# A delta-rule layer in which keys and values are turned by VectorE blocks and SBUF-to-SBUF transfers instead of TensorE transposes

## The chip, the cores and the metric

The kernel runs on one core of a Trainium2 chip. The metric is device time in microseconds (us), smaller is better. The kernel before took 1355.09 us (median of 3 runs, 1355.00 to 1355.52). Everything is float32.

## The reference

Two layers over 1152 token positions of width 1024: a prompt of 1024 tokens and eight sampled sequences of 16 tokens. Layer 0 (a linear recurrence beside windowed attention) is not touched. Layer 1 is a gated delta rule with 8 heads of 128 key and 128 value channels. Cut to what matters:

```python
qkv, z, b, a = split(hmod @ w_in)            # 3072 + 1024 + 8 + 8 channels
qkv = silu(causal_dwconv(qkv))               # 4 taps along the tokens
q, k = l2_normalize(q) * 128 ** -0.5, l2_normalize(k)
beta, g = sigmoid(b), -exp(a_log) * softplus(a + dt_bias)
# per chunk: A = (k beta) k^T * decay_strict ; T = (I + A)^-1
w, u, qk = T @ (k beta exp(gcum)), T @ (v beta), (q k^T) * decay_incl
# scan over the chunks
v_new = u - w @ state
o     = (q exp(g)) @ state + qk @ v_new
state = state * exp(g_last) + (k exp(g_last - g))^T @ v_new
y = (rms_norm(o) * silu(z)) @ w_out
```

The kernel writes this for chunks of 128 tokens, which gives the same result: 8 prompt chunks and one that holds all the samples, so 9 in a head.

## The kernel before, in words

The output of the projection lies with channels on the partitions and tokens along them. `S1` holds three such planes of 128x1152 for one head: keys, queries, values (`KEY`, `QUERY`, `VALUE` = 0, 1, 2). Products over channels (`gram_tiles`, `pairs`) take their operands from `S1` directly. Two operands are needed with the tokens on the partitions: `KD` (keys times a decay, nine tiles of 128x128) is the stationary operand of the state update in `scan`, and `VB` (values times a factor `vs`) is the right-hand side of the triangular solve. Before the change TensorE turns them: `transposes` writes 9 tiles of keys (`turn_k` five of them, `extra(1)` in `rest` four) and 9 of values (`extra(6)`, `extra(7)`, `extra(8)`) into PSUM, 18 in each head; VectorE takes them out and scales them, in `keys(h, 0..2)` and `values(h, 0..2)`. A third family of transposes, `outputs`, turns the result back, 9 in a head, and stays.

Each engine has one written program, in which all heads run the same order: `rest(h)` (five rounds of an inverse of 32x32 blocks by powers, then two steps up to 64 and 128), `scan(h)` (eight dependent chunk steps, k = 0 to 7), and then the start of the next head (`gram_k`, on VectorE `front`, `keys`, `norm_q`). Between these dependent pieces stands filler, in 39 numbered places p: on TensorE `fill(h, p)` issues two or three matmuls of the next head's input projection (128x128 by 128x288), whose halves use two PSUM banks in turn; `between(h, p)` on VectorE and ScalarE does the additions, convolution taps and activations that belong to them. `TAIL` is the last four places. The value plane of a head is finished late: its last taps are at p = 0 to 2, ScalarE's tanh at p = 3 and VectorE's `silu(h, VALUE)` at p = 5, that is after the third round of `rest(h)`. The first use of `VB` is the first matmul of `scan(h)`, at k = 0.

SyncE issues every DMA from one queue in written order, and a semaphore wait there holds up all that follows. For head h: the weights of head h + 1, then (after the first step of the scan) the convolution history, the decay rows and the remaining weights, then the sample states. In the last head (h = 7, `ahead` false) it loads `w1out[3]` to `w1out[6]` first, four pieces of 512 KB of the output projection. They lie in the buffers `CV` and `U1` of the convolution; at p = 4 of that head TensorE begins the output projection (`share`), and its first `share` waits for all seven pieces. GpSimd's program for `rest(h)` is: small copies of decays, one weight sum, then, when the fifth round is done, six copies into `XW` and `YF`, in head 0 also the difference `TD4`, and then `head_sums(h + 1, 1)`, the weight sums of the next head's second half.

Of the kernel before, what the change touches and what calls it, by code (L numbers as in the profile page):

```python
# [18 lines left out]
ALU = mybir.AluOpType  # L19
# [3 lines left out]
P = 128  # L23
# [275 lines left out]
def encoder(nc, I, O):  # L299
    ctx = ExitStack()  # L300
    with ctx:
# [173 lines left out]
        TD4 = HT[:, 0:HALF, LO:]  # L475
        zt_half = zt.rearrange("p a t -> p (a t)")[:, 0:LO]
# [36 lines left out]
        def _(sp):  # L513
# [65 lines left out]
            for m in range(LM):  # L579
                if m:  # L580
                    sp.wait_ge(sem("l_mm"), 6 * m)
                sp.dma_start(gw, I["gw"][m]).then_inc(sem("gw_in"), 16)
# [9 lines left out]
            sp.dma_start(wqkv, I["wqkv"]).then_inc(sem("wqkv_in"), 16)  # L592
# [14 lines left out]
            sp.dma_start(kc, I["kc"]).then_inc(sem("kc_in"), 16)  # L607
# [103 lines left out]

            def head(h, ahead):
                if not ahead:
                    for k in range(3, KT - 1):
                        sp.wait_ge(sem("s1_ready"), 3 * H - 2 if k < 5 else 3 * H - 1)
                        sp.dma_start(w1out[k], I["wout"][1, :, k]).then_inc(sem("wout1_in"), 16)
                if ahead:
                    sp.wait_ge(sem("n_ev1"), 7 * h + 4)
# [5 lines left out]
                    weights(h + 1, 3)  # L724
                sp.wait_ge(sem("st_ready"), 8 * h + 1)
                if not ahead:
                    sp.wait_ge(sem("s1_ready"), 3 * H)
                    sp.dma_start(w1out[KT - 1], I["wout"][1, :, KT - 1]).then_inc(sem("wout_in"), 16)
# [66 lines left out]
        def _(pool):  # L795
# [226 lines left out]
            def rest(h, ahead):  # L1022
                wait(pool, sem("kd_ready"), 3 * h + 1)
# [106 lines left out]
        def _(pe):  # L1130
# [159 lines left out]
            def gates(m):  # L1290
                pe.wait_ge(sem("gw_in"), 16 * m + 16)
# [11 lines left out]
                for q in range(2):  # L1303
                    pe.wait_ge(sem(f"w0_in{q}"), 16 * m + 48)
                    project(m, q, "g_mm", lambda n: pe.wait_ge(
# [3 lines left out]
            pe.wait_ge(sem("wqkv_in"), 16)  # L1309
# [93 lines left out]
            def att(t):  # L1403
# [17 lines left out]
                if sample:  # L1421
                    pe.wait_ge(sem("kc_in"), 16)
# [234 lines left out]
            def transposes(bank, m, ks, name, at=0):  # L1657

                for i, k in enumerate(ks):
                    x = tr(at_(bank, at + i), col(m, k))  # L1660
                x.then_inc(sem(name), 1)

# [19 lines left out]
            def turn_k(h):  # L1682
                if not (isinstance(h, int) and h == 0):
                    pe.wait_ge(sem("y1_done"), 3 * h - 1)
                transposes(2, 0, range(4), "tk")
                transposes(4, 0, (8,), "tk")

            def rest(h, ahead):
# [4 lines left out]
                def extra(n):  # L1693
# [4 lines left out]
                    elif n == 1:  # L1698
                        if not first:
                            wait(pe, sem("y1_done"), 3 * h)  # L1700
                        transposes(3, 0, hi, "tk")
                        pe.wait_ge(sem("kd_ready"), 3 * h + 2)
# [3 lines left out]
                    elif n == 3:  # L1706
                        pe.wait_ge(sem("kd_ready"), 3 * h + 3)
# [87 lines left out]
            def scan(h, ahead):  # L1795
                for k in range(8):
# [8 lines left out]
                    else:  # L1805
                        pe.wait_ge(sem("n_ev1"), 7 * h + 7)
                        pe.wait_ge(sem("vb_ready"), 3 * h + 3)
# [17 lines left out]
                    pe.wait_ge(sem("vn_ready"), 8 * h + k + 1)  # L1825
                    mm(at_(6, 2), KD[:, k], VN, start=True, stop=True).then_inc(sem("kv_mm"), 1)
# [1660 lines left out]
```

## Time and profile before

| | |
|---|---|
| median of 3 runs | 1355.09 us |
| profiled execution, span | 1354.8 us |
| TensorE matmul busy | 1325.8 us, 98% |
| TensorE weight load busy | 904.0 us, 67% |
| VectorE busy | 855.6 us, 63% |
| ScalarE busy | 434.6 us, 32% |
| GpSimd busy | 331.1 us, 24% |
| DMA | 111.96 MB in 63297 packets |
| mean granted TensorE clock | 0.997 of full speed |

The span is the time from the first to the last instruction of one profiled execution. Every matmul is issued by one helper line (L1132) and every transpose by another (L1135), so groups of TensorE are told apart by the shape. A matmul of float32 shows as two records, a transpose as one. Busy time of TensorE counts from issue to a modelled end, and records of neighbours overlap: 98% means that it nearly always had something in flight. In the timelines neighbouring instructions of one line are merged in one row. The head's period is read from VectorE's L3188, which runs once in each head: at 671.37, 756.89 and 842.40 us.

### The profile page before, as it was taken

To read this page: it belongs to the slowest core of one execution; us is meant where nothing else is said; L and a number is where in the kernel's file an instruction comes from. 1 tells how busy PE (TensorE), PEld (TensorE's weight loads), DVE (VectorE), ACT (ScalarE), POOL (GpSimd) and SP (SyncE) were. 2 spreads that over 40 slices of the span, in tenths; PEclk is the share of its full clock that TensorE was granted. 3 is DMA by queue.
4 is the path that set the end of the run, shared out by engine and by line. 5 is a ranking of instruction groups with operands and counts; after the bars stand their busy time and mean duration, and the time that the engine had idled before them with its cause. 6 is when DMAs were issued, how large, how long until landed. Compare 5 with 4: busy or idle time off the path is not lost.

```text
span 1354.8 us, 27409 instructions
## 1 busy us (share of the span) xinstructions
PE 1325.8 (98%) x11200; PEld 904.0 (67%) x11200; DVE 855.6 (63%) x1939; ACT 434.6 (32%) x1044; POOL 331.1 (24%) x450
## 2 busy tenths in 40 slices
PE   5999999999999999999999999999999999999997
PEld 3577776666654454667877788877788777875543
DVE  3847874355454375785886858858578586782246
ACT  3213443344431233521422414224143241432221
POOL 1023200010013232523312423224222242212352
PEclk9999999999999999999999999999999999999999
DMA  9531016002034522121212112121121211440124
GB/s 356 235 75 36 5 36 271 8 1 79 3 130 167 195 85 108 13 81 19 71 46 68 34 34 83 38 77 40 34 83 29 75 50 34 127 159 26 35 94 168
DMA packets 63297, 111.96 MB, mean 83 GB/s; under 512 B 34778, under 2 KB 38690, under 8 KB 61618
## 3 DMA queue, kind: packets, MB, share of 16 engines
q1 hardware_dynamic: 63172, 110.21, 24.2%
q8 instruction: 89, 1.46, 0.4%
q14 instruction: 36, 0.29, 0.1%
HBM read 91.79 MB, written 18.40 MB: 81 GB/s over the span
## 4 chain that ended last, share of the span: by engine, by line
PE 88%; DVE 7%; POOL 1%; DMA 1%; issue 1%; ACT 1%; SPq 0%; DVEq 0%; POOLq 0%; ACTq 0%
PE psum L1132 83%; PE psum L1135 5%; DVE mem L2963 1%; DVE mem L2774 1%; DVE mem L3288 1%; DMA mem<-x_dram 1%; DVE mem L3054 0%; DMA y<-mem 0%; DVE mem L3165 0%; DVE mem L2943 0%; DMA mem<-x 0%; POOL mem L954 0%; DVE mem L2780 0%; ACT mem L1915 0%; ACT mem L2087 0%
## 5 line engine op out<-in xcount | busy, mean ns | idle before, releaser
L1132 PE MATMUL psum<-mem 32*32 32x32 f32 (+12 forms) x10592 | 1264.1, 304 | 4.9 <-DVE mem L2475 1.5
L1132 PEld LDWEIGHTS psum<-mem 128*128 128x128 f32 (+4 forms) x10592 | 835.7, 143 | 401.7 <-issue 217.0
L2963 DVE SCALAR_TENSOR_TENSOR mem<-mem 128x576 f32<-128x576 f32 (+1 forms) x126 | 106.1, 842 | 0.0
L1135 PE MATMUL psum<-mem 128*128 128x128 f32 (+1 forms) x608 | 85.1, 278 | 17.2 <-ACT mem L1927 12.9
L1135 PEld LDWEIGHTS psum<-mem 128*128 128x128 f32 (+1 forms) x608 | 70.7, 144 | 41.4 <-issue 21.0
L2278 ACT ACTIVATE mem<-mem 128x128 f32<-128x128 f32 x72 | 22.0, 305 | 127.6 <-DVE mem L3213 74.4
L2164 ACT ACTIVATE mem<-psum 128x288 f32<-128x288 f32 x28 | 11.4, 407 | 104.0 <-PE psum L1132 104.0
L1011 POOL COPY mem<-mem 128x3 f32<-128x3 f32 x24 | 8.4, 348 | 148.9 <-DVE mem L2921 70.1
L2056 ACT ACTIVATE mem<-mem 128x256 f32<-128x256 f32 x72 | 35.5, 495 | 26.4 <-DVE mem L2697 26.4
L2744 DVE TENSOR_TENSOR mem<-mem,psum 128x512 f32<-128x512 f32 x28 | 19.1, 684 | 37.4 <-PE psum L1132 37.0
L2174 ACT ACTIVATE mem<-mem 128x576 f32<-128x576 f32 (+1 forms) x42 | 32.7, 779 | 28.0 <-DVE mem L2941 28.0
L2682 DVE CUSTOM_DVE_ANT_0 mem<-psum,mem 128x256 f32<-128x256 f32 x72 | 26.2, 419 | 23.4 <-PE psum L1132 23.4
L985 POOL TENSOR_TENSOR mem<-mem 128x512 f32<-128x512 f32 x14 | 15.2, 1088 | 103.8 <-issue 93.3
L2087 ACT ACTIVATE mem<-mem 128x1024 f32<-128x1024 f32 x16 | 16.9, 1056 | 71.5 <-DVE mem L2744 30.3
L2204 ACT ACTIVATE mem<-mem 128x1176 f32<-128x1176 f32 x24 | 28.3, 1178 | 30.2 <-DVE mem L2963 30.2
L2987 DVE SCALAR_TENSOR_TENSOR mem<-mem 128x1024 f32<-128x1024 f32 (+1 forms) x31 | 36.7, 1185 | 0.4 <-ACT mem L2204 0.3
L865 POOL TENSOR_TENSOR mem<-mem 128x512 f32<-128x512 f32 x8 | 9.9, 1268 | 109.9 <-DVE mem L2682 108.7
L1927 ACT ACTIVATE mem<-mem 128x1024 f32<-128x1024 f32 x18 | 20.5, 1144 | 48.6 <-POOL mem L806 26.2
L3174 DVE SCALAR_TENSOR_TENSOR mem<-psum,mem 128x128 f32<-128x128 f32 x56 | 19.4, 346 | 25.4 <-PE psum L1132 25.4
L2774 DVE SCALAR_TENSOR_TENSOR mem<-mem 128x1024 f32<-128x1024 f32 x16 | 20.5, 1281 | 19.7 <-POOL mem L856 14.4
L3190 DVE COPY mem<-psum 128x128 f32<-128x128 f32 x64 | 18.4, 287 | 21.0 <-PE psum L1132 20.9
L3205 DVE SCALAR_TENSOR_TENSOR mem<-mem,psum 128x128 f32<-128x128 f32 x56 | 19.2, 344 | 17.1 <-PE psum L1132 17.1
(260 smaller groups left out, 1277.2 us busy)
## 6 DMA issues: line engine op xcount, KB each, us to landing
mem<-modw SPq DMA_DIRECT2D x12, 2048.0 KB, 12.2
mem<-w SPq DMA_DIRECT2D x44, 512.0 KB, 4.3
mem<-x SPq DMA_DIRECT2D x10, 512.0 KB, 4.7
x_dram<-mem SPq DMA_DIRECT2D x9, 512.0 KB, 2.9
mem<-row_dram SPq DMA_DIRECT2D x8, 576.0 KB, 5.2
mem<-x_dram SPq DMA_DIRECT2D x9, 512.0 KB, 3.7
mem<-wout SPq DMA_DIRECT2D x1, 4096.0 KB, 15.0
mem<-gs SPq DMA_DIRECT2D x8, 512.0 KB, 3.6
```

The lines of the kernel that those rows point to most:

```text
L1132: return pe.matmul(*a, **k)
L1135: return pe.transpose(out, in_, ident[0:n, 0:n])
L1927: act.activation(xh[:, slot], XS[:, t % XSLOTS] if l else X[:, t], ACT.Copy, scale=stat[:, 3 * slot + 2:3 * slot + 3]).then_inc(sem("n_xh" ...
L2056: c.mark(act.activation(SS[:, a], SS[:, a], ACT.Exp, scale=HD ** -0.5, bias=nm[:, a:a + 1], accum_out=den[:, a:a + 1]))
L2174: act.activation(CV[:, m, lo:hi], U1[:, m, lo:hi], ACT.Copy, scale=CW[:, 3 * g + ORDER[m], 0:1]).then_inc(sem("pj_ev"), 1)
L2204: act.activation(U1[:, m, PRE:], CV[:, m, 0:UC], ACT.Tanh, scale=0.5).then_inc(sem("th1"), 1)
L2278: x = act.activation(SQJ, OO[:, k], ACT.Square, accum_out=sso[:, k:k + 1])
L2682: i = dve.tensor_tensor_reduce(SS[:, n], B(bk)[:, a * 256:(a + 1) * 256], mask, 1.0, -3.0e38, ALU.add, ALU.max, mx[:, n:n + 1])
L2774: i = dve.scalar_tensor_tensor(two(tmp), src, rs, two(gate[:, w]), ALU.mult, ALU.mult)
L2963: x = dve.scalar_tensor_tensor(cvm, U1[:, m, lo + j:hi + j], CW[:, 3 * g + ORDER[m], j:j + 1], cvm, ALU.mult, ALU.add)
L2987: dve.scalar_tensor_tensor(S1[:, m, a:b], T[:, a:b], 1.0, CV[:, m, a:b], ALU.add, ALU.mult)
L3174: dve.scalar_tensor_tensor(RR, at_(6, 0), HC[:, 1, k:k + 1], VB[:, k], ALU.mult, ALU.add).then_inc(sem("r_ready"), 1)
```

## The change

After the change no TensorE transposes of keys and values are left. In their place: VectorE transposes each plane in 32x32 blocks in one instruction (keys into `KB`, values into `VT`, both in the convolution buffer `CV`); SyncE then moves block row a of each tile to block column a with sixteen SBUF-to-SBUF transfers a plane, each of 32 partitions x 9 tiles x 128 bytes (36 KB); then `KD` is scaled in place by ScalarE (nine instructions of 128x128) and `VB` by GpSimd (one of 128x1152). Several semaphores of layer 0 are merged with others, which changes names and counts only.

```diff
+        KB, VT = CV[:, KEY, 0:TOK], CV[:, VALUE, 0:TOK]
...
             def head(h, ahead):                                   # SyncE
+                sp.wait_ge(sem("kb_ready"), h + 1)
+                if h:
+                    sp.wait_ge(sem("kv_mm"), 8 * h)
+                    sp.wait_ge(sem("sample_mm"), 4 * h)
+                turned(KD, KB, "kd_in")
                 if not ahead:
-                    for k in range(3, KT - 1):
+                    for k in (4, 5, 6, 3):
+                        if k == 3:
+                            sp.wait_ge(sem("kd_in"), 256 * H)
                         sp.wait_ge(sem("s1_ready"), 3 * H - 2 if k < 5 else 3 * H - 1)
                         sp.dma_start(w1out[k], I["wout"][1, :, k]).then_inc(sem("wout1_in"), 16)
                 if ahead:
-                    sp.wait_ge(sem("n_ev1"), 7 * h + 4)
...
+                sp.wait_ge(sem("vt_ready"), h + 1)
+                if h:
+                    sp.wait_ge(sem("o_tp"), 3 * h)
+                turned(VB, VT, "vb_in")
                 sp.wait_ge(sem("st_ready"), 8 * h + 1)
...
+            def turned(dst, src, name):
+                for a in range(4):
+                    for b in range(4):
+                        sp.dma_start(dst[32 * b:32 * b + 32, :, 32 * a:32 * a + 32],
+                                     src.rearrange("p (c t) -> p c t", t=P)[32 * a:32 * a + 32, :,
+                                                                            32 * b:32 * b + 32]
+                                     ).then_inc(sem(name), 16)
...
             def rest(h, ahead):                                   # GpSimd, after the copies into YF (and TD4)
+                wait(pool, sem("vb_in"), 256 * (h + 1))
+                wait(pool, sem("vs_ready"), h + 1)
+                pool.tensor_tensor(VB, VB, bc(vs, 2, P), ALU.mult).then_inc(sem("vb_ready"), 1)
                 if ahead:
                     head_sums(h + 1, 1)
...
-            def turn_k(h):                                        # TensorE
-                if not (isinstance(h, int) and h == 0):
-                    pe.wait_ge(sem("y1_done"), 3 * h - 1)
-                transposes(2, 0, range(4), "tk")
-                transposes(4, 0, (8,), "tk")
...
                     elif n == 1:
                         if not first:
-                            wait(pe, sem("y1_done"), 3 * h)
-                        transposes(3, 0, hi, "tk")
-                        pe.wait_ge(sem("kd_ready"), 3 * h + 2)
+                            wait(pe, sem("y1_done"), 3 * h - 1)
                         pairs(4, 0, 1, (8,), "gq_mm", 2)
...
                     elif n == 3:
-                        pe.wait_ge(sem("kd_ready"), 3 * h + 3)
+                        if not first:
+                            wait(pe, sem("y1_done"), 3 * h)
                         pairs(3, 0, 0, hi, "gram_mm")
...
-                    elif n == 6:
-                        pe.wait_ge(sem("umf_ready"), 2 * h + 2)
-                        pe.wait_ge(sem("s1_ready"), 3 * h + 3)
-                        transposes(3, 2, lo, "tv")
-                    elif n == 7:
-                        pe.wait_ge(sem("eq_ready"), 3 * h + 2)
-                        transposes(4, 2, hi, "tv")
-                    else:
-                        pe.wait_ge(sem("eq_ready"), 3 * h + 3)
-                        transposes(2, 2, (8,), "tv")
...
+            def scaled_keys(h):                                   # ScalarE, after between(h, 5)
+                wait(act, sem("kd_in"), 256 * (h + 1))
+                wait(act, sem("kb_ready"), h + 1)
+                for k in range(NT):
+                    i = act.activation(KD[:, k], KD[:, k], ACT.Copy, scale=kdc[:, k:k + 1])
+                i.then_inc(sem("kd_ready"), 1)
...
-            def keys(h, n):                                       # VectorE
-                a, b, src = ((0, 4, four(2)), (8, 9, four(4, 0, 1)), (4, 8, four(3)))[n]
-                dve.wait_ge(sem("tk"), 3 * h + n + 1)
-                if n == 0:
-                    c.sync()
-                dve.tensor_tensor(KD[:, a:b], src, bc(kdc[:, a:b], 2, P), ALU.mult
-                                  ).then_inc(sem("kd_ready"), 1)
+            def keys(h):
+                dve.wait_ge(sem("s1_ready"), 3 * h + KEY + 1)
+                dve.transpose(KB, S1[:, KEY]).then_inc(sem("kb_ready"), 1)
...
+            def values(h):                                        # VectorE, at p == 5 right after silu(h, VALUE)
+                dve.wait_ge(sem("s1_ready"), 3 * h + VALUE + 1)
+                dve.transpose(VT, S1[:, VALUE]).then_inc(sem("vt_ready"), 1)
```

## Rows read from the trace of the kernel before

**Rows 1.** The page: busy time by engine, and the chain that ended last by engine
```profile
PE 1325.8 (98%) x11200; PEld 904.0 (67%) x11200; DVE 855.6 (63%) x1939; ACT 434.6 (32%) x1044; POOL 331.1 (24%) x450
...
PE 88%; DVE 7%; POOL 1%; DMA 1%; issue 1%; ACT 1%; SPq 0%; DVEq 0%; POOLq 0%; ACTq 0%
```

**Rows 2.** Busy time in one head's period: stretch, its length, engines, clock, DMA, GB/s
```profile
671.37:756.89 85.52, 85.08 (x1071) 67.46 (x1070) 63.21 (x147) 27.04 (x75) 24.05 (x38) 1.00 0.19 54
```

**Rows 3.** TensorE's transposes in that period: busy, mean ns of one | idle before
```profile
L1135 PE MATMUL psum<-mem 128*128 128x128 f32 x27 | 4.2, 275 | 0.3 <-DVE mem L3165 0.3
```

**Rows 4.** Chain of waits, 690 to 725: start, us, what
```profile
692.09 0.66 PE psum L1135 x4
...
708.47 0.44 PE psum L1135 x4
708.91 1.46 PE psum L1132 x6
```

**Rows 5.** VectorE's timeline at the start of a head: start, us, instruction [idle before]
```profile
681.95 0.46 DVE L3032 TENSOR_TENSOR mem<-psum,mem 128x288 f32<-128x288 f32 x1 [0.19 <-PE psum L1132]
...
686.34 0.89 DVE L3054 TENSOR_TENSOR mem<-psum,mem 128x512 f32<-128x512 f32 x2
...
690.93 0.48 DVE L3092 STREAM_TRANSPOSE mem<-mem 128x288 f32<-128x288 f32 x1
...
700.21 0.22 DVE L3105 TENSOR_TENSOR mem<-mem,psum 128x64 f32<-128x64 f32 x1 [1.82 <-PE psum L1132]
```

**Rows 6.** VectorE's timeline from the value plane to the scan's first copy
```profile
703.33 2.15 DVE L2987 SCALAR_TENSOR_TENSOR mem<-mem 128x1024 f32<-128x1024 f32 x1
705.41 0.28 DVE L2993 SCALAR_TENSOR_TENSOR mem<-mem 128x128 f32<-128x128 f32 x1
706.45 0.46 DVE L3112 TENSOR_TENSOR mem<-mem,psum 128x288 f32<-128x288 f32 x1 [0.77 <-PE psum L1132]
...
723.03 0.29 DVE L3190 COPY mem<-psum 128x128 f32<-128x128 f32 x1 [0.37 <-PE psum L1132]
```

**Rows 7.** SyncE's timeline: issues of small transfers, alone and close together
```profile
556.38 0.43 SPq L686 DMA_DIRECT2D mem<-lmask  x1
556.85 0.43 SPq L687 DMA_DIRECT2D mem<-ident  x1
...
726.31 1.64 SPq L676 DMA_DIRECT2D mem<-cs  x3
727.99 2.14 SPq L699 DMA_DIRECT2D mem<-row_dram  x1
```

**Rows 8.** The page's DMA issues: KB each, us from issue to landing
```profile
mem<-wout SPq DMA_DIRECT2D x8, 512.0 KB, 5.9
...
mem<-cs SPq DMA_DIRECT2D x28, 12.0 KB, 2.4
...
mem<-lmask SPq DMA_DIRECT2D x4, 20.0 KB, 1.8
```

**Rows 9.** GpSimd's timeline: the difference of head 0, and the copies into YF of head 2
```profile
629.84 5.05 POOL L1046 TENSOR_TENSOR mem<-mem 128x2304 f32<-128x2304 f32 x1
...
713.48 1.81 POOL L1040 COPY mem<-mem 32x288 f32<-32x288 f32 x4
```

**Rows 10.** ScalarE's timeline: four 128x128 scalings, and its copy of round 4
```profile
684.61 1.28 ACT L2239 ACTIVATE mem<-mem 128x128 f32<-128x128 f32 x4 [0.61 <-DVE mem L3042]
...
705.83 0.41 ACT L2250 ACTIVATE mem<-psum 128x288 f32<-128x288 f32 x1 [2.21 <-PE psum L1132]
```

**Rows 11.** Last head: SyncE's four loads
```profile
1197.62 2.30 SPq L716 DMA_DIRECT2D mem<-wout  x4
```

**Rows 12.** Last head: VectorE's timeline at its key copies and its third round
```profile
1197.25 0.89 DVE L3054 TENSOR_TENSOR mem<-psum,mem 128x512 f32<-128x512 f32 x2
...
1209.16 0.21 DVE L3105 TENSOR_TENSOR mem<-mem,psum 128x64 f32<-128x64 f32 x1
```

**Rows 13.** Busy time and DMA rate while those loads move
```profile
1199.00:1205.00 6.00, 5.76 (x113) 4.47 (x99) 5.90 (x13) 0.69 (x1) 0.00 (x0) 1.00 1.02 408
```

More of the change, by code:

```diff
@@ L1022, in rest @@
             def rest(h, ahead):
-                wait(pool, sem("kd_ready"), 3 * h + 1)
+                wait(pool, sem("kb_ready"), h + 1)
                 c.mark(pool.tensor_copy(HC, HCn[:, 1:3]))
@@ L1290, in gates @@
             def gates(m):
-                pe.wait_ge(sem("gw_in"), 16 * m + 16)
+                pe.wait_ge(sem("proj_in"), 16 * m + 16)
                 pe.wait_ge(sem("xc_ready"), m + 1)
@@ L1655, in gram_tiles @@
                 return x
[L1657 to L1661, printed above, removed]
             def pairs(bank, m, n, ks, name, at=0):
@@ L1825, in scan @@
                     pe.wait_ge(sem("vn_ready"), 8 * h + k + 1)
+                    if k == 0:
+                        pe.wait_ge(sem("kd_ready"), h + 1)
                     mm(at_(6, 2), KD[:, k], VN, start=True, stop=True).then_inc(sem("kv_mm"), 1)
@@ L1989, in lru @@
                     if m and i == 0:
-                        wait(act, sem("l_a"), m)
+                        wait(act, sem("l_act"), 2 * m - 1)
                     elif m and i == 3:
@@ L2005, in lru @@
                 wait(act, sem("l_w"), m + 1)
-                act.activation(lw_, lw_, ACT.Sqrt).then_inc(sem("l_sq"), 1)
+                act.activation(lw_, lw_, ACT.Sqrt).then_inc(sem("l_act"), 1)
                 if m == LM - 1:
                     for g in range(6):
-                        wait(act, sem("g_mm"), g + 1)
+                        wait(act, sem("xa_mm"), 6 + g + 1)
                         wait(act, sem("g_ev"), G_LAST + g - 1)
@@ L2170, in first_tap @@
                 wait(act, sem("s1_ready"), 3 * (g - 1) + m + 1)
+                if m == KEY:
+                    wait(act, sem("kd_in"), 256 * g)
+                elif m == VALUE:
+                    wait(act, sem("vb_in"), 256 * g)
                 if n:
@@ L2253, in rest @@
                     between(h, 2 * r - 1, ahead)
+                    if r == 3:
+                        scaled_keys(h)
                 between(h, 8, ahead)
@@ L2596, in chain @@
             def chain(m):
-                dve.wait_ge(sem("l_a"), m + 1)
+                dve.wait_ge(sem("l_act"), 2 * m + 1)
                 dve.wait_ge(sem("lz_ev"), 6 * m + 6)
@@ L2607, in chain @@
                     added(m + 1, "u2")
-                dve.wait_ge(sem("l_sq"), m + 1)
+                dve.wait_ge(sem("l_act"), 2 * m + 2)
                 c.sync()
@@ L3026, in between @@
                     silu(h, VALUE)
+                    values(h)
             def front(h):
@@ L3067, in norm_q @@
                        sem("ssq_ready"), h + 1)
-            def values(h, n):
-                a, b, src = ((0, 4, four(3)), (4, 8, four(4)), (8, 9, four(2, 0, 1)))[n]
-                dve.wait_ge(sem("tv"), 3 * h + n + 1)
-                if n == 0:
-                    dve.wait_ge(sem("vs_ready"), h + 1)
-                dve.tensor_tensor(VB[:, a:b], src, bc(vs[:, a:b], 2, P), ALU.mult
-                                  ).then_inc(sem("vb_ready"), 1)
+            def values(h):
+                dve.wait_ge(sem("s1_ready"), 3 * h + VALUE + 1)
+                dve.transpose(VT, S1[:, VALUE]).then_inc(sem("vt_ready"), 1)
             def queries(h, n):
@@ L3129, in rest @@
                         queries(h, 2)
-                    else:
-                        values(h, 1)
                     between(h, 2 * r - 2, ahead)
@@ L3135, in rest @@
                             norm_q(0)
-                        keys(h, 2)
                     elif r == 2:
@@ L3140, in rest @@
                         queries(h, 1)
-                    elif r == 4:
-                        values(h, 0)
-                    else:
-                        values(h, 2)
                     if r < 5:
@@ L3236, in head @@
                     between(h, TAIL + 1, ahead)
-                    keys(h + 1, 0)
-                    keys(h + 1, 1)
+                    keys(h + 1)
                     between(h, TAIL + 2, ahead)
@@ L3260, in _ @@
                         conv(7, j)
-            keys(0, 0)
-            keys(0, 1)
+            keys(0)
             for h in range(H - 1):
```

25 lines of the change are left out of this document (13 added, 12 removed).

## The prediction

> **What bounds the kernel now.** I read the page's busy times and its chain first: TensorE has something in flight for 98% of the span and holds 88% of the chain that ended last, VectorE 7% [rows 1]. Then the stretches: in a head's period of 85.52 us TensorE is busy for 85.08, VectorE for 63.21, and the granted clock is 1.00, the upper of its two levels (2.4 GHz) [rows 2]. So the delta layer costs about what TensorE's instruction stream costs, and each instruction taken from it is worth its issue interval, not its duration. The groups show the difference: 27 transposes in the period, mean 275 ns each, yet 4.2 us of busy time in all [rows 3]. The chain gives the interval: 0.44 us for four in a row, so 0.11 for one; a record of a filler matmul takes 1.46 / 6 = 0.24 [rows 4].
>
> The Trainium skill (Perfetto Trace Analysis, "Identifying the Most-Contended Engine") says that matmul busy time is a poor measure of TensorE's load and weight-load busy time a better one; that stands at 67% here. By that rule TensorE would have slack, and removed transposes would be worth nothing. What bears against it is in the chain, which by the next paragraph leaves TensorE only at the head's start.
>
> There VectorE is the one that is late. From 681.95, when it stops waiting for TensorE, it works without a gap, and TensorE waits for its L3165 until 692.09 [rows 4, 5], by 0.3 us on the matmul side [rows 3]. VectorE first idles again at 700.21 [rows 5]. After that TensorE leads through the rest of the period: VectorE waits at 706.45 and at 723.03 [rows 6].
>
> **The change part by part**, for head 2 (671.37 to 756.89), in the clock of the kernel before.
>
> Key transposes. Nine go, 9 x 0.11 = 0.99 us, and with them the wait on L3165 (0.3), now needed only two places later: at most 1.3. But VectorE sets the end here. Its two copies `keys(h, 0)` and `keys(h, 1)` took 0.89 [rows 5]. The block transpose of 128x288 took 0.48 [rows 5]. The one of 128x1152 is not in this trace. Bounds: four times the small one, 1.9, and from below the 0.89 that those copies took for 640 columns. VectorE's pace is (0.46 - 0.29) / (288 - 128) = 0.00106 us for a further column (L3032 and L3190) [rows 5, 6], which makes 0.48 + 864 x 0.00106 = 1.4; I take that, since a long instruction is mostly streaming. So VectorE comes 0.5 us later to the round-1 transpose, which ended at 691.41 [rows 5] and now ends at 691.9. TensorE's second round starts then. Before, it started at 692.09 + 0.44 + 0.22 (one pair, two records of a size like a transpose) = 692.75. Gain 0.8 us at each of the seven starts that have a head before them, 5.6. With a transpose of 1.9 us it is 0.3 each, 2.1. Head 0 has TensorE in the lead, so all nine count: 1.0.
>
> Value transposes. Nine in `rest`, where TensorE leads: 0.99 x 8 heads = 7.9 us. `values(h)` puts 1.4 us on VectorE after `silu`, which ended at 705.69 [rows 6]; 0.8 earlier plus 1.4 gives 706.3. The queue behind it is round 4 (L3112 at 706.45, or 705.65 with the gain) [rows 6], so that starts 0.65 late. TensorE has six filler matmuls of two records each between rounds 4 and 5 (12 x 0.24 = 2.9 us) [rows 4], which cover it. If the cover fails it costs 0.7 us a head.
>
> Getting `VB` in time. This is the new path: block transpose done 706.3, sixteen DMA issues, landing, one GpSimd multiplication, then TensorE's first matmul of the scan. That one ran just before VectorE's copy at 723.03 [rows 6], at about 722.6; with 1.8 us gained it wants `VB` at 720.8.
> - Issue: small transfers follow each other at 0.47 us (556.38, 556.85) [rows 7], three with many 12-byte pieces at 0.55, and the next behind those took 2.14 [rows 7], so (1.64 + 2.14) / 4 = 0.95 is the bound above. Each new one has 288 pieces of 128 bytes; the `lmask` one has 160 of that size and is the nearest row. I take 0.47: the last is issued at 706.3 + 15 x 0.47 = 713.4.
> - Landing: 1.8 us for `lmask`, 2.4 for `cs` [rows 8]. I take 2.1: 715.5. No transfer from SBUF to SBUF is in the trace; the same pair serves as bounds.
> - GpSimd: its copies end at 715.3, less the gain, so it is free [rows 9]. 128x2304 took 5.05 us [rows 9], so 128x1152 takes about 2.6: `VB` is ready at 718.1.
> That leaves 2.7 us: nothing is added. The decisive number is the issue interval: at (720.8 - 2.6 - 2.1 - 706.3) / 15 = 0.65 us the slack is gone, and at 0.95 TensorE waits 4.5 us in each head.
> Behind this wait on GpSimd stand the weight sums `head_sums(h + 1, 1)`, which TensorE's filler first wants at place 25, in the scan's fifth step, some 15 us later. On SyncE, history and rows wait for the scan's first state anyway; the loads of weights in front lose a wait and go earlier.
> In head 0 the difference `TD4` (5.05) stands ahead of the multiplication [rows 9]: it ended at 634.89, now about 1 us earlier, plus 2.6 is 636.5. TensorE wants `VB` at 722.6 less a period of 85.5 less the 2.0 of its 18 transposes, 635.1. Cost 1.4 us, once.
>
> `KD`. Block transpose ends at 686.34 + 1.4 = 687.7, the sixteen issues at 695.2, landed 697. ScalarE scales after place 5, nine at 0.32 = 2.9 us [rows 10], from about 702.6 to 705.5; behind it stands its copy for round 5, at 705.83 [rows 10], used only some 3 us later. `KD` itself is first read in the scan. Nothing added; at 0.95 a transfer it lands at 704.1, and the copy would be 2 us late, still inside the cover.
>
> The last head. SyncE issues the keys' sixteen transfers ahead of the four `wout` loads. Before, these were issued from 1197.62 [rows 11] and moved at 408 GB/s in a stretch that ended near 1206 [rows 13]. Now `KB` is ready at 1197.25 + 1.4 = 1198.6 [rows 12], the transfers are out at 1206.2, the first three loads at 1207.4, and the fourth waits for the keys to land, 1208.1. Four times 524 KB at 408 GB/s is 5.1 us, so all have landed at about 1213.2. TensorE's first `share` comes right after round 3, whose result VectorE took at 1209.16 [rows 12], so at 1209.0, less 0.8: 1208.2. It waits 5.0 us, once. Bounds: 2.5 us if most of the loads overlap the keys' transfers, 9 with slow issues.
>
> Sum: -5.6 - 1.0 - 7.9 + 1.4 + 5.0 = -8.1 us. The profiled span 1354.8 becomes 1346.7; the median stands 0.3 above the span, so 1347.0.
>
> **A rule that speaks against it.** Small transfers close together overlap in this trace: each landed 1.8 us after its issue while the next was out 0.47 us later [rows 7, 8]. The Trainium skill (DMA: Bandwidth & Descriptors, "Rules for kernel authors") says to coalesce many small transfers, since under 64 KB one pays mostly overhead. With the fixed 2.0 us that its section on the anatomy of one DMA gives for the GpSimd path, taken one after the other, a plane would need some 32 us and each head would lose about 20, an estimate. The first rival below goes the same way, by rows.
>
> **The rivals.**
> 1. `VB` late, slower. Place: TensorE's first matmul of every scan. Price: the issue interval above 0.65 us, times 15. For it: the pieces are 128 bytes on both sides, nearly twice as many as in the nearest row, and 2.14 us behind the `cs` burst [rows 7]. Against: `lmask` has the same piece size and kept 0.47. At 0.8 us each: landing at 720.4, ready 723.0, 2.2 us in each of eight heads (18 more, less the 1.4 that head 0 has anyway), and 5 more in the last head: 1347 + 16 + 5 = 1368. At 0.95: 1347 + 35 + 7 = 1389.
> 2. Everything hidden. The loads of the last head overlap, and VectorE's longer chain does not show: 15.8 us for 144 transposes and up to 2.1 for seven waits, less the 1.4 of head 0: 1338 to 1341. For it: TensorE's 98%. Against: VectorE's chain at the start has no idle time to give [rows 5].
> 3. TensorE doesn't lead, as the weight-load share suggests: the gains of the value part vanish in waits between rounds. -5.6 - 1.0 + 1.4 + 5.0 = -0.2, about 1355, and 1353 to 1357 with a part of them kept or a wait added.
>
> **How the numbers follow.** My forecast, 1347 with its own range of 1342 to 1352: 0.57. Rival 1: 0.24, slower than before from about 0.70 us an issue on. Rival 2: 0.10. Rival 3: 0.09, of it 0.08 within 0.2% (2.7 us, about what a measurement of this kernel can tell from no change). The mild end of rival 1 and the slow end of the forecast give the same again or less. Faster 0.67, same 0.09, slower 0.24. The range: 1339 to 1371, which leaves about 0.1 above and little below.
>
> **What would show it.** The period of L3188 falls from 85.5 to 83.7 us. SyncE's row of sixteen issues is 7.5 us long, 9.5 at most. TensorE has no wait on GpSimd at the scan's first matmul except in head 0, and one of about 5 us before the first `share`. The second round's start follows VectorE's L3092 directly. The forecast is wrong if a plane's transfers take over 10 us from first issue to landing plus 2, if the block transpose takes over 2 us, or if the period does not shrink.

## The result and the profile after

The changed kernel takes 1363.55 us (median of 4 runs, 1362.64 to 1368.9) against 1355.3 in the same session. The ratio is 1.007, with a 95% interval of 1.0053 to 1.0088: slower. 1347.0 was forecast, faster.

The page of the changed kernel, answering to [rows 1]:

```profile
PE 1311.3 (96%) x11056; PEld 889.1 (65%) x11056; DVE 852.5 (63%) x1907; ACT 455.0 (33%) x1116; POOL 352.4 (26%) x458
...
DMA packets 141122, 121.41 MB, mean 89 GB/s; under 512 B 112602, under 2 KB 116514, under 8 KB 139442
...
PE 82%; DVE 5%; issue 4%; SPq 3%; DMA 2%; POOL 2%; ACT 0%; POOLq 0%; DVEq 0%; ACTq 0%
```

TensorE has lost 144 records and 14.5 us of busy time, and the span has still grown by 7.2 us (8.3 by the medians: the traced execution of before is 1.5 us longer than its usual ones, as shown below). SyncE's queue, 0% of the chain before, holds 3% of it, which is some 40 us. The waits of TensorE (us in total, times, longest) name what took the gain:

```profile
PE psum L1156 <- DMA mem<-wout: 11.6, 1, 11.6
PE psum L1156 <- POOL mem L1070: 9.0, 6, 2.3
```

L1156 issues the matmuls and L1070 is GpSimd's scaling of `VB`. In before's trace TensorE waits for neither. Both waits begin at SyncE. Its timeline in head 2 (as the prediction calls the second of the eight, h = 1) and in the last head, a plane's sixteen transfers in a row:

```profile
685.93 12.11 SPq L717 DMA_DIRECT2D mem<-mem  x16
...
704.29 12.06 SPq L717 DMA_DIRECT2D mem<-mem  x16
...
1194.33 12.82 SPq L717 DMA_DIRECT2D mem<-mem  x16
1207.20 2.03 SPq L733 DMA_DIRECT2D mem<-wout  x4
```

and one issue by itself (ns, min/median/max), where [rows 7] had 0.43 us for `lmask`:

```profile
L717 SPq DMA_DIRECT2D mem<-mem x256: 585/613/1797, 601.1 to 1234.8; - x128
```

Most take 0.61 us and one to four in each plane 0.7 to 1.8, so that a plane costs 10.9 to 12.8 us, 11.9 in the mean, or about 0.75 a transfer. The long ones have a companion in the trace. All 27 issues over 1 us overlap a 16 KB transfer of the queue that the page calls `instruction` (q8, the loading of code), and most of them end 0.4 us behind its end. Of the 224 issues up to 0.7 us only 28 overlap one. One of the long issues, and the DMA view of 707 to 708:

```profile
707.55 1.11 SPq L717
...
q8 instruction: 1, 0.02, 6.0%
```

The chain of waits in head 2 (start, us, what) shows how that reaches TensorE:

```profile
702.88 1.39 DVE mem L3087
704.27 0.02 issue
704.29 0.60 SPq L717
...
711.29 6.63 issue
...
717.97 2.09 POOL mem L1070
720.06 0.14 issue
720.20 4.04 PE psum L1156 x30
```

GpSimd has nothing to do for 6.6 us and starts when the last transfer has landed. The same view for the last head, and then TensorE around that stall (stretch, length, busy, granted clock, DMA share, GB/s):

```profile
1208.33 0.43 SPq L733
...
1208.86 6.33 DMA mem<-wout
1215.18 0.14 issue
1215.32 14.74 PE psum L1156 x179
```
```profile
1194.00:1204.00 10.00, 9.64 (x249) 1.00 0.52 133
1204.00:1215.30 11.30, 0.00 (x0) 0.69 0.61 202
1215.30:1219.00 3.70, 3.68 (x7) 0.56 0.00 0
1219.00:1223.00 4.00, 4.00 (x101) 1.00 0.00 0
```

After the stall TensorE runs at half the clock, the lower of its two levels, until 1218.5. For 3.2 us of work that costs another 1.6 us (an estimate).

Where the time went, by the start of the line that [rows 2] runs between (L3188, now L3193), the head's mark:

| | before | after | kernel without transfers (e1) |
|---|---|---|---|
| start to head 0's mark | 671.4 | 669.8 | 667.5 |
| six middle periods, mean | 85.2 | 84.7 | 82.9 |
| last period | 90.2 | 101.3 | 89.7 |
| last mark to the end | 82.3 | 82.5 | 82.1 |

The third mark of before is at 841.98, not at 842.40 as said above: of its periods the first is 85.5 us and the other five are 85.1.

2.0 us of the first row belong to none of the heads, nor to the change. Near the start TensorE has a wait of 0.5 us for VectorE, which is the same in every kernel. It ends at 47.35 in before's trace, at 45.39 in the changed kernel's and at 45.23 in e1's. Before's execution had its first load later (TensorE's first wait ends at 10.33 instead of 9.44) and then a stretch at half the clock:

```profile
25.90:29.30 3.40, 3.00 (x5) 1.82 (x6) 1.42 (x4) 2.39 (x5) 0.75 (x3) 0.50 1.02 430
```

e2's execution has such a stretch too, and 19 other executions of before have a median span of 1353.3 us, not 1354.8. From the end of that wait to head 0's mark it is 624.0 us before, 624.4 after and 622.3 in e1.

The price of the transfers by the medians is 1363.6 - 1338.8 = 24.8 us. The waits for `VB` (9.0), the one for `wout` (11.6) and the half clock behind it (1.6) make 22.2. What is left is spread: middle periods less their waits are still 0.2 to 0.4 us above e1's. Its cause stays open.

### The profile page after: what moved, and what is told of

Its sections match the earlier page's. It is cut to its first block, busy times and chain, and to the rows that moved or that the text cites. A ratio compares the mean times of both kernels' runs of the same rounds, so it can differ in the third digit from the quotient of the medians.

```text
span 1362.0 us, 27447 instructions
## 1 busy us (share of the span) xinstructions
PE 1311.3 (96%) x11056; PEld 889.1 (65%) x11056; DVE 852.5 (63%) x1907; ACT 455.0 (33%) x1116; POOL 352.4 (26%) x458
## 4 chain that ended last, share of the span: by engine, by line
PE 82%; DVE 5%; issue 4%; SPq 3%; DMA 2%; POOL 2%; ACT 0%; POOLq 0%; DVEq 0%; ACTq 0%
PE psum L1156 79%; PE psum L1159 3%; SPq L717 3%; DMA mem<-modw 2%; POOL mem L1070 1%; DVE mem L3002 1%; POOL mem L1061 1%; DVE mem L3070 1%; DVE mem L3087 1%; DMA mem<-wout 0%; DVE mem L2978 0%; POOL mem L1067 0%; DVE mem L3094 0%; DVE mem L3061 0%; DVE mem L3058 0%
## 5 line engine op out<-in xcount | busy, mean ns | idle before, releaser
L1156 PE MATMUL psum<-mem 32*32 32x32 f32 (+12 forms) x10592 | 1261.6, 304 | 29.6 <-DMA mem<-wout 11.6
L1156 PEld LDWEIGHTS psum<-mem 128*128 128x128 f32 (+4 forms) x10592 | 837.4, 143 | 435.0 <-issue 244.6
L1159 PE MATMUL psum<-mem 128*128 128x128 f32 (+1 forms) x464 | 62.6, 279 | 14.1 <-ACT mem L1928 12.2
L1159 PEld LDWEIGHTS psum<-mem 128*128 128x128 f32 (+1 forms) x464 | 53.3, 145 | 30.0 <-issue 18.6
L2165 ACT ACTIVATE mem<-psum 128x288 f32<-128x288 f32 x28 | 11.5, 409 | 95.4 <-PE psum L1156 95.4
L2759 DVE TENSOR_TENSOR mem<-mem,psum 128x512 f32<-128x512 f32 x28 | 19.2, 685 | 37.3 <-PE psum L1156 36.9
L1006 POOL TENSOR_TENSOR mem<-mem 128x512 f32<-128x512 f32 x14 | 15.2, 1089 | 89.1 <-issue 79.6
L2789 DVE SCALAR_TENSOR_TENSOR mem<-mem 128x1024 f32<-128x1024 f32 x16 | 20.5, 1281 | 18.8 <-POOL mem L877 14.7
```

The lines of the kernel that those rows point to most:

```text
L1156: return pe.matmul(*a, **k)
L1159: return pe.transpose(out, in_, ident[0:n, 0:n])
L2789: i = dve.scalar_tensor_tensor(two(tmp), src, rs, two(gate[:, w]), ALU.mult, ALU.mult)
```

## The experiments

My theory: the transposes were worth what the prediction says or more, but sixteen issues in a row hold SyncE's queue for 12 us instead of 7.5, and this (a) makes `VB` late and (b) puts the last head's `wout` loads far behind TensorE. Rivals: TensorE doesn't lead; the DMA engines and not the queue are the limit; the pieces and not the transfers set the issue time.

**e1, no transfers.** VectorE writes the turned 32x32 blocks straight into `KD` and `VB` (float32 as before, though the text below calls the planes bf16). The blocks stay where they are, so this kernel's results are other ones, as are those of e3, e5 and e10:

```
-                turned(KD, KB, "kd_in")
-                turned(VB, VT, "vb_in")
-                dve.transpose(KB, S1[:, KEY]).then_inc(sem("kb_ready"), 1)
+                dve.transpose(flat(KD), S1[:, KEY]).then_inc(sem("kb_ready"), 1)
```
(the values likewise; the waits for the transfers go)

> VectorE turns the 32x32 blocks of keys and values straight into the bf16 planes and no SBUF-to-SBUF transfer is issued; the blocks stay where they are, so the planes hold values in other places and the arithmetic is that of other numbers. 144 TensorE transposes are gone, as in the changed kernel, and SyncE's queue is that of before. Theory A (TensorE's work sets the end; the SyncE queue took the gain back): the periods of the middle heads fall by the prediction's 0.8 + 0.99 = 1.8 us, the end of the last head stays as before, and the time is 1355.3 - 14.5 to 16 = 1339 to 1341 us. Theory B (the transposes lie in holes of TensorE, so that taking them out gives nothing): 1353 to 1356 us. Theory C (only the keys' transposes, ahead of an empty pipeline, count): 1347 to 1349 us.

1338.8 us, ratio to before 0.9872 (0.9857 to 0.9887). Theory A. Its period, which answers to [rows 2]:

```profile
667.50:750.40 82.90, 82.67 (x1053) 65.75 (x1052) 62.46 (x142) 29.55 (x84) 26.69 (x39) 1.00 0.19 55
```

Its six middle periods lie between 82.90 and 82.97. So 18 transposes a head are worth 2.2 us there. In the last head only 0.5 us show. There TensorE has a stall of 1.3 us at 1190.13 for which the profile shows no releaser.

**e2, the last head's loads first.**

```
+                if not ahead:
+                    for k in (4, 5, 6):
+                        sp.wait_ge(sem("s1_ready"), 3 * H - 2 if k < 5 else 3 * H - 1)
+                        sp.dma_start(w1out[k], I["wout"][1, :, k]).then_inc(sem("wout1_in"), 16)
                 sp.wait_ge(sem("kb_ready"), h + 1)
...
                 turned(KD, KB, "kd_in")
...
+                q = (0, 1, 2, 4, 5, 6, 3)[k]
```

> The changed kernel, but in the last head three of the four wout loads stand ahead of the keys' sixteen transfers in SyncE's queue, and the fourth, which needs the place of the weights' last reader, behind them; TensorE takes that tile last. Theory A (the last period's extra 11 us is wout issued 12.8 us later): TensorE's 11.6 us wait for wout falls to under 1.5 us, the last period falls from 101.3 to 90 to 92 us, and the time is 1363.6 - 10 = 1352 to 1355 us. Theory B (the last head is slow because the transfers of 128-byte pieces crowd wout's own transfer on the DMA engines, whatever the order): the landing grows by several us, and the time is 1359 to 1363 us.

1351.7 us, ratio 0.9972 (0.9958 to 0.9987): this edit alone makes the change a gain. The last period is 91.2 us, and TensorE waits:

```profile
PE psum L1158 <- POOL mem L1071: 5.9, 6, 1.7
...
PE psum L1158 <- DMA mem<-wout: 1.8, 1, 1.8
```

Theory A, though the wait that is left is 1.8 us where under 1.5 was said, and the time is just below its range. Three of the four loads went forward, and the fourth stays behind the keys. Of the 11.8 us, 10.1 are in the last period. The rest is in heads that this edit doesn't touch: the same program waited 9.0 us for `VB` in the one execution and 5.9 in the other. Such waits are compared below with that in mind.

**e3 and e10, what makes an issue slow.** Sixteen transfers and 36 KB each stay. e3 takes 32 pieces of 1152 bytes, e10 all 128 partitions and 128 pieces of 288:

```
e3  +  sp.dma_start(dst.rearrange("p c t -> p (c t)")[32 * b:32 * b + 32, 32 * NT * a:32 * NT * (a + 1)],
    +               src[32 * a:32 * a + 32, 32 * NT * b:32 * NT * (b + 1)])
e10 +  sp.dma_start(dst.rearrange("p c t -> p (c t)")[:, n:n + 72], src[:, n:n + 72])
```

> The changed kernel with the same 16 transfers a plane of 36 KB each, but every one made of 32 pieces of 1152 bytes instead of 288 of 128; the data land in other places of the planes, so the arithmetic is that of other numbers. Theory A (what a transfer costs SyncE grows with the number of its pieces): one issue goes from 0.65 us (585 to 1797 ns) to the 0.47 us of the cs, lmask and ident loads, a plane from 12.1 to 7.5 us, the wait for the values' plane (9.0 us in sum over six heads) is gone, the last head's wait falls from 11.6 to about 7, and the time is 1347 to 1351 us. Theory B (a transfer from SBUF to SBUF costs SyncE 0.65 us whatever its pieces, or a queue of sixteen backs up): the issue stays at 0.6 to 0.7 us, and the time is within 1361 to 1364 us.

> The changed kernel with the same 16 transfers of 36 KB a plane, but each from all 128 partitions to the same 128, 72 columns wide (128 pieces of 288 bytes); the arithmetic is that of other numbers. Theory A (a transfer from SBUF to SBUF costs SyncE 0.6 us and more, whatever its shape): the issue stays at 0.59 to 0.61 us, a plane at 11 to 12 us, and the time is 1358 to 1364 us. Theory B (what makes the issue slow is that 32 partitions are read and 32 written): one issue takes 0.43 to 0.47 us as those of the loads from DRAM, a plane takes 7.5 to 8 us, the values' plane is in time, and the time is 1347 to 1351 us.

e3: 1358.2 us (ratio 1.0018, 1.0009 to 1.0027); e10: 1360.0 (1.0036, 1.0019 to 1.0053). Their issues:

```profile
L717 SPq DMA_DIRECT2D mem<-mem x256: 507/591/1748, 601.9 to 1227.0; - x128
```
```profile
L718 SPq DMA_DIRECT2D mem<-mem x256: 465/601/1804, 601.1 to 1230.8; - x128
```

A ninth of the pieces takes 0.02 us off the median, and 0.7 us off a plane in the mean of all sixteen (11.2 instead of 11.9; e10: 11.4). The long ones stay, and again all of them overlap a load of code. For e3 theory B is near: the shape matters little. Its time lies between both forecasts, and its waits for `VB` are 3.6 us instead of 9.0 or 5.9: near the edge of the slack a little less counts for much. For e10 theory A.

**e5, four transfers instead of sixteen**, with the same 4608 pieces of 128 bytes in a plane:

```
+                    sp.dma_start(dst[:, :, 32 * a:32 * a + 32],
+                                 src.rearrange("p (c t) -> p c t", t=P)[:, :, 32 * a:32 * a + 32]
```

> The changed kernel with 4 transfers a plane instead of 16: each moves all 128 partitions of a quarter of the columns, 1152 pieces of 128 bytes, so bytes and pieces of a plane are what they were, and the partitions stay, so the arithmetic is that of other numbers. Theory A (SyncE pays by the transfer, some 0.65 to 0.75 us each): a plane takes 2.6 to 3.0 us of the queue instead of 12.1, the values' plane is never late (9.0 us back), wout is issued 9 us sooner (its 11.6 us wait falls to 2 or 3), and the time is 1342 to 1347 us. Theory B (SyncE pays by the piece): one issue grows to 2.5 to 3 us, the plane stays at 11 to 12 us, and the time is 1360 to 1364 us. Theory C (the DMA engines are what a plane waits for): the issues are short and the landing grows to 8 us or more, and the time is 1350 to 1360 us.

1347.2 us, ratio 0.9935 (0.9922 to 0.9949). TensorE waits for GpSimd nowhere, the middle periods are 82.9 us as in e1, and `wout` costs 6.0 us. SyncE's planes in head 2, and one issue:

```profile
685.41 3.44 SPq L716 DMA_DIRECT2D mem<-mem  x4
...
703.76 3.08 SPq L716 DMA_DIRECT2D mem<-mem  x4
```
```profile
L716 SPq DMA_DIRECT2D mem<-mem x64: 595/744/3166, 602.5 to 1209.2; - x64
```

Four times the pieces in a transfer raise its median from 0.61 to 0.74, so a plane falls to a quarter. Theory A, at the slow edge of its range. As equal bytes in equal pieces are in time here, the DMA engines were not the limit for `VB` (that the partitions stay doesn't matter, by e10). The landing grew from 2.1 to 3.8 us, which is hidden there. In the last head it is not: one issue took 3.2 us, and the fourth load waits for the keys' landing (4.0 us), so that TensorE's wait is 6.0 us where 2 to 3 was said.

**e4 and e9, the keys alone.** The values go back to TensorE's transposes, with `wout` behind the keys (e4) or ahead of them (e9):

```
-                turned(VB, VT, "vb_in")
+                    elif n == 6:
+                        pe.wait_ge(sem("umf_ready"), 2 * h + 2)
+                        pe.wait_ge(sem("s1_ready"), 3 * h + 3)
+                        transposes(3, 2, lo, "tv")
```
(and the rest of `values(h, n)` as before)

> The keys are turned by VectorE and sixteen transfers as in the changed kernel; the values go through TensorE's transposes and VectorE's scaled evictions as in the kernel before. Theory A (the values' transfers give back per head what their transposes gained, and the keys' the last head's wait): no wait for the values' plane, the middle periods are 85.1 - 0.8 = 84.3 us, the last period is 90.2 - 0.8 + 11 = about 100 us, and the time is 1355.3 - 6.6 + 11 = 1359 to 1361 us. Theory B (it is the values' transfers that delay the last head): the last period is under 92 us, and the time is 1348 to 1351 us.

> Only the keys are turned by VectorE and sixteen transfers, the values go through TensorE's transposes as before, and in the last head three wout loads stand ahead of the keys' transfers. Theory A (the values' plane is the one that a slow queue makes late, the keys' is in time once wout is out of its way): the middle periods are 83.9 us as with the keys alone, TensorE's 11.5 us wait for wout is gone, and the time is 1359.7 - 11 = 1347 to 1350 us, below the 1351.7 of the version that turns both with sixteen transfers: turning the values so loses. Theory B (the keys' transfers have a price of their own in the last head beside wout): 1352 us or more.

e4: 1359.7 us, ratio 1.0031 (1.002 to 1.0042), periods of 83.9 us but one (85.7, with a stall of 1.6 us without a releaser), the last 102.6, and

```profile
PE psum L1148 <- DMA mem<-wout: 11.5, 1, 11.5
```

Theory A. e9: 1350.5 us, ratio 0.996 (0.9945 to 0.9974), just above A's 1350; the last period is 90.9, but one middle period is 87.6 (last section). That turning the values too (e2, 1351.7) loses against leaving them is not shown: they were measured apart, and their ratios to before (0.9972 and 0.996) have intervals that overlap. What is shown: with sixteen transfers the values gain nothing that can be measured, and in the changed kernel's order of loads they lose: 1363.55 us against e4's 1359.7, with ratios whose intervals lie apart.

**e6, two queues.** Half of the values' transfers from ScalarE, on top of e2:

```
+                for a in (2, 3):
+                    for b in range(4):
+                        act.dma_start(VB[32 * b:32 * b + 32, :, 32 * a:32 * a + 32], ...)
                 wait(act, sem("w_mm"), L + 2)
```

> The kernel with the wout loads ahead of the keys' transfers, and half of the values' sixteen transfers issued by ScalarE, which idles for 6 us there, beside SyncE's half. Theory A (the plane is late by the time that one queue needs for sixteen issues): the values' plane lands some 6 us sooner, TensorE's wait for GpSimd's scaling (5.9 us in six heads) is gone, each middle period is at most 84 us, and the time is 1351.7 - 6 to 8 = 1344 to 1346 us. Theory B (two queues share what makes the issues slow, so that 8 beside 8 take as long as 16): 1350 to 1352 us. Theory C (ScalarE's eviction behind the issues comes late): a wait of TensorE for ScalarE appears, and the time is above 1352 us.

1349.95 us, ratio 0.9954 (0.9942 to 0.9967). The wait for GpSimd is gone, and another stands in its place:

```profile
703.59 6.84 ACTq L2289 DMA_DIRECT2D mem<-mem  x8
710.48 0.38 ACT L2294 ACTIVATE mem<-psum 128x256 f32<-128x256 f32 x1 [7.49 <-issue]
```
```profile
PE psum L1167 <- ACT mem L2294: 3.7, 5, 1.0
```

SyncE's eight took 5.9 us beside it, 0.74 each as when alone, so theory B's mechanism falls, though its 1350 is the nearest number. But the long issues are shared: in each of the first seven heads both queues have one at the same time, and both end within 0.02 us (in head 2, SyncE's 1.28 us at 708.84 and ScalarE's 1.63 us at 708.83). Theory C's mechanism came with a total that A and C both missed: ScalarE's eight issues took 6.8 us of a hole of 6.1, and the eviction behind them, for the inverse's step up to 64, came late by up to 1 us.

**e7 and e8, the changed kernel's planes with fewer issues**, both on top of e2. e7 writes the plane to DRAM and reads it back in four; e8 lets GpSimd copy the four blocks of the diagonal and issues twelve:

```
e7 +                sp.dma_start(t_dram[n], src).then_inc(sem(f"t_out{n}"), 16)
   +                sp.wait_ge(sem(f"t_out{n}"), 16 * (h + 1))
   +                for b in range(4):
   +                    sp.dma_start(dst[32 * b:32 * b + 32].rearrange("p c (a t) -> p c a t", t=32),
   +                                 t_dram[n].rearrange("(a p) (c b t) -> b p c a t", p=32, b=4, t=32)[b])
e8 -                    for b in range(4):
   +                    for b in (b for b in range(4) if b != a):
   +                for q in range(4):
   +                    r = slice(32 * q, 32 * q + 32)
   +                    pool.tensor_copy(dst[r, :, r], src.rearrange("p (c t) -> p c t", t=P)[r, :, r])
```

> The kernel with the wout loads ahead of the keys' transfers, and each plane turned through DRAM: one transfer writes it out, four read it back in pieces of 128 bytes, 5 issues instead of 16. Theory A (the number of issues is what costs): issues 5 times 0.65 and two landings of 2.1 us make 7.5 us from VectorE's transpose to the last landing instead of 14.2, the values' plane is not late, and the time is 1344 to 1347 us. Theory B (the trip through DRAM costs more than eleven issues): the landings are 4 us and more each, the plane is as late as before or later, and the time is 1351 us or more.

> The kernel with the wout loads ahead of the keys' transfers; the four blocks on each plane's diagonal, which need no change of partition, are copied by GpSimd, and 12 transfers a plane are left. Theory A (the queue's time is by the transfer): a plane takes 9 us of the queue instead of 12.1, the values' plane is 3 us sooner, half or more of TensorE's 5.9 us wait goes, and the time is 1346 to 1349 us. Theory B (GpSimd's eight small copies a head push its other work back): TensorE or VectorE waits for GpSimd, and the time is 1351 to 1356 us.

e7: 1341.3 us, ratio 0.9893 (0.9878 to 0.9908), middle periods of 82.9. e8: 1341.4, 0.9891 (0.9878 to 0.9905), middle periods of 83.0 to 83.3. Theory A in both, and better than it said. For e7 the way to it was longer than theory A had it: from the first issue in head 2 to the last landing it is 10.6 us, not 7.5, since the write takes 2.8 to land and the reads 4.1. That is still in time. The values' planes in head 2, e7 and then e8:

```profile
702.71 0.33 SPq L718 DMA_DIRECT2D t_dram<-mem  x1
705.53 3.89 SPq L724 DMA_DIRECT2D mem<-t_dram  x4
```
```profile
702.64 9.41 SPq L717 DMA_DIRECT2D mem<-mem  x12
```

In e8 GpSimd's scaling starts at 713.62, 11.0 us after SyncE's first issue, and in after 13.7. Those 2.7 us are more than `VB` was ever late (2.3); its copies (2.3 us a plane) fell into idle time.

**e11, through DRAM, but `wout` last:** e7's transfers on the changed kernel's order of loads.

> Both planes turned through DRAM in 5 issues, and the last head's wout loads left behind the keys' plane, as in the changed kernel. Theory A (the late wout is a matter of how long the queue is held, and its wait costs TensorE's clock besides): the queue is held from the keys' transpose for 0.4 us, a landing of 2 to 3 us and four issues of 3.4 us, some 6.5 us instead of 12.8; TensorE waits 5 to 6 us for wout instead of 11.6, the middle periods stay at 82.9 us, and the time is 1341.3 + 4 to 6 = 1345 to 1347 us. Theory B (with the planes' traffic out of the way, wout's place in the queue no longer matters): 1341 to 1342 us.

1350.0 us, ratio 0.9955 (0.994 to 0.997). I had expected 1345 to 1347. SyncE is at `wout` 10.0 us after the keys' transpose instead of 12.9, but in the last head the write to DRAM takes 6.5 us to land, where it is 2.8 to 4.4 for the keys elsewhere, and the four `wout` loads take 3.8 us to issue. TensorE waits 10.1 us, and then it runs at half the clock:

```profile
1192.00:1202.00 10.00, 0.40 (x1) 0.59 0.79 241
1202.00:1208.00 6.00, 6.00 (x15) 0.55 0.00 0
1208.00:1215.00 7.00, 7.00 (x184) 1.00 0.22 86
```

Half the clock until 1207.4 costs 2.9 us here (an estimate) where the changed kernel lost 1.6, so the last period, 101.0 us, is nearly as long as its 101.3. So it is loads queued behind a plane, and not the sixteen issues in themselves, that this head cannot bear.

**e12, the best of each:** keys as in e8, values as in e7.

> wout ahead of the keys' transfers; the keys turned by 12 transfers and GpSimd's four diagonal copies, the values through DRAM in 5 issues. Theory A (each plane is in time, and what is left above the kernel without transfers are GpSimd's copies of the values, 0.24 us a period, and the last head's landing of the keys behind wout in DRAM, 1.4 us): 1339.5 to 1341 us. Theory B (what is left has nothing to do with how the planes travel): 1341.3 us as with either alone.

1339.1 us, ratio 0.9879 (0.9864 to 0.9894): below both kernels of the case and level with e1 (which has that stall of 1.3 us). Its last period is 89.1 us, no wait for `wout` appears, and the middle periods are 83.0 to 83.3. So theory A's number was nearly met and both of its terms were wrong. The 1.4 us in the last head are not there, and the 0.2 us a period are, though the values go as in e7. They come with the keys' way, twelve transfers and GpSimd's copies. Which of the two it is was not separated.

## Why the prediction was wrong

The failed step is one line of "Getting `VB` in time": issue interval "I take 0.47", from the `lmask` row. It measured 0.65 with its gap, and 0.75 with the long ones. The text gave 0.65 as the point where the slack is gone. That interval entered twice. Beside it the sum put the half clock behind the last head's wait at nothing, without a reason: 1.6 us.

- `VB`. In time since the head's mark: forecast 34.9 us for the block transpose's end, 44.1 for the last landing, 46.7 for `VB` ready, 49.4 for TensorE's need. Measured in head 2: 34.5, 48.2, 50.3 and 48.9 (720.20 less the wait of 1.5). The last issue comes 11.5 us behind the first instead of 7.1, landing was right (2.1), GpSimd's multiplication was 0.5 shorter than said. TensorE waited 9.0 us in six heads where 1.4 in one was forecast. e5 and e7 take the cause away, and their middle periods are e1's.
- Head 0. The forecast 1.4 us, for `TD4` ahead of the multiplication, were 1.7, but that is luck: GpSimd waited for the transfers. Without them (e1) the multiplication follows `TD4` at once and TensorE doesn't wait. After, then e1:

```profile
633.14 2.11 POOL L1070 TENSOR_TENSOR mem<-mem 128x1152 f32<-128x1152 f32 x1 [1.66 <-DMA mem<-mem]
...
630.88 2.11 POOL L1058 TENSOR_TENSOR mem<-mem 128x1152 f32<-128x1152 f32 x1
```
- The last head. Forecast 5.0 us, bounds 2.5 to 9, measured 11.6. From the mark: `KB` ready 16.2 against 16.1, TensorE there 25.8 against 25.5, `wout` landed 30.8 against 36.9. Of these 6.1 us, 5.2 are the issues (12.8 instead of 7.6). The bound "9 with slow issues" was too low by its own rows: at 0.95 us each sixteen issues take 7.7 us more than at 0.47, which with the 5.0 makes 12.7. e2 returns 10.1 us in that period.
- Key transposes. Forecast 0.8 us a head; e4's periods of 83.9 against 85.1 make it 1.2. The block transpose was right (1.4 forecast, 1.37 measured). But VectorE did not come 0.5 us later to the end of round 1's transpose. It ended 20.0 us behind the mark before, 20.5 by the forecast and 20.25 after; the block transpose started 0.2 us sooner than the copies did. That is 0.3 of the 0.4 us:

```profile
689.52 0.48 DVE L3104 STREAM_TRANSPOSE mem<-mem 128x288 f32<-128x288 f32 x1
```
- Value transposes. Forecast 0.99 us a head; 83.9 (e4) less 82.9 (e1) is 1.0.
- TensorE leads. Right: e1's 1338.8 is the rival "everything hidden" (1338 to 1341), 16.6 us below before. 144 issue intervals are 15.8, and the waits for VectorE at the heads' starts fell from 2.0 to 1.4, so the removed instructions were worth their issue interval. The weight-load share of 67% did not mean slack.
- `KD`. Nothing was added in the middle heads, as forecast: with the keys alone (e4) TensorE waits for no plane.
- Rival 1 named place and mechanism, with a chance of 0.24. Its price at 0.8 us each was 1368, against 1363.6 at 0.75. Its wait of 2.2 us in each of eight heads was too high, since only six waited, by 0.4 to 2.3; the last head's 5 more was near the 6.6 more that were measured. So the place and the order of size of what came stood in the text. What was wrong is the side of 0.65 us on which the number was put.

The Trainium skill (DMA: Bandwidth & Descriptors, "Rules for kernel authors") says to coalesce many small transfers. The runs agree on the transfers: from sixteen (e2) to five (e7) is 1351.7 to 1341.3 us. They don't agree with my use of it, where landings follow one another: each landed 2.1 us after its issue while the next was issued 0.65 us later, and it was the issues that could not overlap.

What I should have seen in the rows: the `cs` burst had 0.55 us and 2.14 behind it, the `lmask` row 0.43, and `VB`'s slack ended at 0.65. The 2.14 (727.99 to 730.13) overlaps a load of code too, so it was a sign of the long ones. With a decisive number that sits inside its own bounds, 0.24 for the far side is too little, and the same number decides the last head too.

## What to carry to other kernels

Here a small SBUF-to-SBUF transfer cost its queue about 0.6 to 0.75 us in each of four shapes, so count the issues in a row and set that time, not the landing, against the slack of who waits. Before a burst goes into a queue, look at every load behind it in every head: the one exceptional head had 11.6 us of waiting and 1.6 us of half clock here, `VB` 9.0 us of waiting in all the others together. Work taken off the leading engine is worth its interval, but only as long as what replaces it has less latency than the slack.

## What the runs showed of the hardware

- SyncE's issue of a transfer from SBUF to SBUF takes 0.59 to 0.61 us in the median for 32, 128 or 288 pieces, and 0.74 for 1152, with single ones up to 2.1 (3.2 for 1152). A plane written to DRAM in 128 pieces of 4608 bytes was issued in 0.33, but twice in 1.3 to 1.5 in e7's last head. What sets 0.6 against 0.33 and the 0.43 of small loads from DRAM stays open.
- Issues over 1 us go with loads of code: 27 of 27 in the changed kernel, 24 of 24 in e2 and in e3, 25 of 25 in e10 and in e8 overlap a 16 KB transfer of the `instruction` queue. Which engine's code it is, and how it holds SyncE up, no run shows. TensorE's stalls of 1.0 to 1.9 us without a releaser (e1, e4, e9 and others) also begin within 0.6 us of the end of such a load.
- A stall of 1.9 us on TensorE was followed in e9 by 3.4 us at half the clock, and that period took 87.6 us instead of 83.9: twice what the stall itself cost. The stall of 1.6 us in e4 had no such stretch behind it, and its period took 85.7.

```profile
954.40:956.40 2.00, 0.13 (x10) 0.05 (x1) 0.00 (x0) 0.22 (x1) 0.00 (x0) 1.00 0.00 0
...
957.80:961.20 3.40, 3.40 (x11) 2.55 (x10) 1.78 (x3) 0.00 (x0) 0.00 (x0) 0.50 0.02 5
```
- VectorE's 32x32 block transpose of 128x1152 float32 took 1.37 us, three times the one of 128x288 for four times the columns. GpSimd's multiplication by a broadcast operand took 2.11 us for 128x1152, where 5.05 for 128x2304 had suggested 2.6.
